# Encoder layer with two attention groups: the sample's queries rounded by GpSimd, its meta weights laid out by VectorE

## The chip, the cores and the metric

The kernel runs as one program on one core of a Trainium2 chip. The metric is the device time of one execution in microseconds (us), given as the median of several runs. The engines are TensorE (PE in the profile; PEld is its weight load), VectorE (DVE), ScalarE (ACT), GpSimd (POOL) and SyncE (SP), whose queue (SPq) issues the DMAs. Each engine works through its own list of instructions in order, and semaphores hold it where it needs another's result.

## The reference

One transformer layer is applied to a prompt of 1024 tokens and, on its own, to a sample of 512 tokens, both of width 1024 and with 16 learned meta tokens in front. Everything is float32.

```python
h = rmsnorm(x, norm1_g)
qa, ka, va, qb, kb, vb = split(h @ w_in)          # 8 heads of group A, 8 query heads of group B
qa, ka, qb, kb = (rmsnorm per head, with gains)
oa = neighbourhood_attn(qa, ka, va, rpb_a)        # 2-D window on the token grid, bias per offset
ob = windowed_gqa(qb, kb, vb, t5_table, sink_b)   # +-128 keys, 2 key heads, bias by distance, sink
x = x + concat(rmsnorm(oa), rmsnorm(ob)) @ w_out
x = x + (silu(h2 @ w_gate) * (h2 @ w_up)) @ w_down    # h2 = rmsnorm(x, norm2_g)
```

In both groups every query also attends to the 16 meta keys: a row of logits is the meta keys, the sink and up to 384 keys of the window. The softmax is taken over all of them together, and the output is the weighted sum of the values, those of the meta tokens included.

## The kernel before, in words

The program goes through stages: norm and projection of three segments of 512 tokens (two of the prompt, one of the sample), with the attention of the prompt behind the second segment and that of the sample behind the third; then the output projection and the feed-forward part for all twelve tiles of 128 tokens. The change lies in the attention of the sample, heads 16 to 31 in the kernel's count: 16 to 23 are group A, 24 to 31 group B. A head of the sample has four tiles of 128 queries, a head of the prompt eight. Tiles are numbered through: the sample's are 128 to 191. A group `g` is four tiles, so one head of the sample.

A float32 product is made exact enough by splitting each operand into a rounded high part (type fp32r) and a low part, the difference. A head's queries are therefore staged twice: the high part `qs[0]` by a copy (`stage_q` on ScalarE, L1251, or `raise_q` on GpSimd, L1001), and the low part by a subtraction (`lower_q` on GpSimd, L1008). The function `q_raised(h)` says which semaphore, and which value of it, tells that the high part of head `h` is there: `q_hi` for ScalarE's, `q_hi_pool` for GpSimd's. In the prompt GpSimd makes the high parts from the third head on. In the sample ScalarE makes all of them: three before the loop, and the other 13 in the loop, behind its work on the third tile of the head two before. When a high part is there, SP copies it by DMA to the other 64 partitions (`double_q`, L826).

For a tile, TensorE makes the scores (`scores`, L1988 to L1991), VectorE adds the bias and takes the maximum (`highest`, L1598), ScalarE the exponential (`exponent`, L1258), TensorE turns the weights (L1995), ScalarE rounds them (`raise_p`, L1267), VectorE makes their low parts (`lower_p`, L1605), and TensorE multiplies by the values (`values`, L2017). The weights of the 16 meta keys go another way, once per group: `keep_meta` (L1059) copies the first 16 columns of four tiles of `logit` into one tile `pmeta` of 64 columns; TensorE turns that (`turn_meta`, L2000), ScalarE and VectorE split it (L1275, L1612), and TensorE multiplies it by a block-diagonal matrix of the meta values (L2028), which GpSimd builds per head (`meta_values`, L1039).

The order on each engine is written out. In the sample GpSimd's turn for head `h` is: the meta weights of head `h - 1`; the masks of head `h + 2` (three additions of 128x256 or 128x384 in group A, L1030; single columns in group B, L1021 and L1022); the low part of the queries of head `h + 2`; the meta values of head `h + 1`; and on odd `h` the scaling of a finished pair of heads (`scale_pair`, L1047):

```python
if h > first:
    keep_meta(H.first // GROUP - 1)
...
if h + ahead < end:
    masks(h + ahead)
...
    lower_q(h + ahead)
if h + 1 < end:
    meta_values(h + 1)
```

SP's turn for head `h` is: the bias rows of head `h + 2` (L813 or L820), `double_q` of head `h + 2`, on even heads the store of a finished pair's sums (L831, behind ScalarE's copy at the head's fourth tile), on odd heads their load back in spread form (L839); four loads of the output weights stand between. TensorE's `turn_meta` for head `h` stands just in front of its scores for head `h + 2`. VectorE's `highest` at the first tile of a head's group waits for `meta_kept`, so that `logit` isn't overwritten early.

Of the kernel before, what the change touches and what calls it, by code (L numbers as in the profile page):

```python
# [19 lines left out]
META = 16  # L20
# [26 lines left out]
GROUP = 4  # L47
# [17 lines left out]
def hybrid_encoder_layer(nc, x_prompt, x_sample, meta_tokens, t5_table, norm1_g, w_in, qn_a_g, kn_a_g,  # L65
# [104 lines left out]
    logit = s("logit", [P, 2 * GROUP, KEYS])  # L170
# [8 lines left out]
    pmeta = s("pmeta", [P, 2, GROUP * META])  # L179
# [58 lines left out]
    with ExitStack() as ctx:  # L238
        bank = [ctx.enter_context(nc.psum_tensor(f"bank{i}", [P, 512], F32)) for i in range(8)]

        def sem(name):
            return ctx.enter_context(nc.semaphore(name))
# [45 lines left out]
        q_hi = sem("q_hi")  # L288
        q_hi_pool = sem("q_hi_pool")
# [5 lines left out]
        expd = sem("expd")  # L295
# [4 lines left out]
        meta_kept = sem("meta_kept")  # L300
        m_turned = sem("m_turned")
        m_hi = sem("m_hi")
        m_lo = sem("m_lo")
        vm_ready = sem("vm_ready")
# [8 lines left out]
        o_scaled = sem("o_scaled")  # L313
# [47 lines left out]
        def wait(eng, s, v):  # L361

            if not isinstance(v, int) or v > 0:
                eng.wait_ge(s, v)
# [19 lines left out]
        def f32(ap):  # L384
            return ap.bitcast(F32)
# [100 lines left out]
        def first_tile(h):  # L486
            return 8 * h if h < 16 else 128 + 4 * (h - 16)
# [122 lines left out]

        def q_raised(h):

            if 2 <= h < 16:
                return q_hi_pool, h - 1
            return q_hi, h + 1 if h < 2 else h - 13

        def double_count(h):

# [358 lines left out]
        def _(pool):  # L977
# [77 lines left out]
            def keep_meta(g):  # L1055
                pool.wait_ge(expd, GROUP * g + GROUP)
                wait(pool, m_turned, g - 1)
                first = GROUP * (g % 2)
                pool.tensor_copy(pmeta[:, g % 2, :].rearrange("p (t m) -> p t m", m=META),  # L1059
                                 logit[:, first:first + GROUP, 0:META]).then_inc(meta_kept, 1)  # L1060

            def attention(seq):
                first, end = HEADS_OF[seq]
                ahead = Head(first).ahead
                lower_q(first)
                pool.wait_ge(att_const, 16 * (first // 16 + 1))
                for h in range(first, first + ahead):
                    masks(h)
                    pool.wait_ge(bias_ready, h + 1)
                    lower_q(h + 1)  # L1070
                meta_values(first)
                for h in range(first, end):
                    H = Head(h)
                    if h > first:
                        keep_meta(H.first // GROUP - 1)
                    raised = first < h < end - ahead and q_raised(h + ahead)[0] is q_hi_pool
                    if raised:
                        pool.wait_ge(meta_kept, H.first // GROUP)
                        raise_q(h + ahead)
                        pool.wait_ge(*q_raised(h + ahead))  # L1080
                    if h + ahead < end:
                        masks(h + ahead)
                    if H.nt > GROUP:
                        keep_meta(H.first // GROUP)
                    if first < h < end - ahead:
                        pool.wait_ge(bias_ready, h + ahead + 1)
                        wait(pool, meta_kept, H.first // GROUP + 1 if H.nt > GROUP else 0)
# [3 lines that stand above are left out]
                    if seq == "prompt" and h % 2 == 0 and h >= 4:  # L1091
                        scale_pair(h // 2 - 2)
                    if h % 2 == 1 and h // 2 - ahead >= first // 2 and (seq == "sample" or h == end - 1):
                        scale_pair(h // 2 - ahead)
                keep_meta(first_tile(end) // GROUP - 1)
                for pair in range(end // 2 - ahead, end // 2):
                    if seq == "sample" and pair == end // 2 - 1:
                        for slot in range(2):
                            mix_lo(0, slot)
                    scale_pair(pair)  # L1100
# [395 lines left out]
        def _(dve):  # L1496
# [104 lines left out]
            def lower_p(n):  # L1601
# [3 lines left out]
                dve.tensor_tensor(turned_to(ptl, n), bank[2 + n % 2][:, 0:k * P].rearrange("p (k c) -> p k c", c=P),  # L1605
                                  f32(turned_to(pth, n)), ALU.subtract).then_inc(p_lo, 1)

            def lower_meta(g):
                pm = pmhl[:, g % 2, :]
                dve.wait_ge(m_hi, g + 1)  # L1610
                dve.wait_ge(p_hi, min(GROUP * g + 6, 128 if g < 32 else 192))
                dve.tensor_tensor(pm[64:P, :], bank[3][0:64, WIN:WIN + P], f32(pm[0:64, :]), ALU.subtract  # L1612
                                  ).then_inc(m_lo, 1)

            def attention(seq):
                n0, n1 = TILES[seq]
                first = HEADS_OF[seq][0]
                for i, q in enumerate(qs[seq]):
                    op = dve.memset(f32(q[1][64 - 64 * (i % 2):P - 64 * (i % 2), :]), 0.0)
                op.then_inc(q_zero, 1)  # L1620
                for h in (first, first + 1):
                    H = Head(h)
                    dve.wait_ge(*q_raised(h))
                    dve.tensor_copy(H.qs[0][H.other, :], H.qs[0][H.own, :]).then_inc(q_twin, 1)
                for h in range(first, first + Head(first).ahead + 1):
                    for k in range(3):
                        b_ = Head(h).bias_kind(k, MK)
                        dve.memset(b_[:, 0:META], 0.0)
                        op = dve.memset(b_[:, META:MK], MASKED)
                op.then_inc(b_zero, 1)  # L1630
                dve.wait_ge(b_zero, 1 if seq == "prompt" else 2)
                for n in range(n0, n1 + 9):
                    if n < n1:
                        highest(n)
                    if n % GROUP == 3 and n0 <= n - 7 < n1:
                        lower_meta((n - 7) // GROUP)
                    if n0 <= n - 2 < n1:
                        lower_p(n - 2)
                        h, t = where(n - 2)
                        if t == Head(h).nt - 1:  # L1640
                            dve.wait_ge(expd, n - 1)
                            wait(dve, rt_turned, h // 2)
                            c = h % 2 * (t + 1)
                            dve.reciprocal(rinv[:, c:c + t + 1], lsum[:, h % 2, 0:t + 1]).then_inc(inv_done, 1)
                    if n % GROUP == 0 and n0 <= n - 12 < n1:
                        h, t = where(n - 12)
                        dve.wait_ge(o_half, (n - 12) // GROUP + 1)
                        for src, dst in Head(h).o_parts(t // GROUP, 0):
                            op = dve.tensor_tensor(dst, src, dst, ALU.add)
                        op.then_inc(o_out, 1)  # L1650
# [604 lines left out]
```

## Time and profile before

| | us |
|---|---|
| median of 3 runs (2011.93 to 2013.73) | 2013.6 |
| the profiled execution | 2009.19 |
| its span, first to last instruction | 2007.4 |
| busy in the span: PE, DVE, ACT, POOL | 1865.8, 1291.5, 997.3, 953.8 |

The span is what the trace covers; the execution's own time has 1.8 us around it. All times in rows count from the span's start. The norm and projection of the prompt run to about 312 us, its attention to about 503, norm and projection of the sample to about 653, the sample's attention to about 768; output projection and feed-forward take the rest. A busy share over the whole span mixes these stages.

### The profile page before, as it was taken

What the parts mean: (1) busy time and instruction counts of PE and PEld (TensorE: products, weight loads), DVE (VectorE), ACT (ScalarE), POOL (GpSimd) and SP (SyncE); (2) the same over time, 40 slices, a digit from 0 to 9 for tenths busy, and PEclk for the clock granted to TensorE, in tenths of its full rate; (3) what the DMA queues carried; (4) which work ended last, traced back from release to release, by engine and by line L of the source; (5) the groups of instructions that cost most, each with busy time, mean ns of one, the idle gap of its engine ahead of it and who ended that gap; (6) DMA issues with size and microseconds to landing.
All of it is one profiled execution on the core that took longest, in us unless ns stands there. A gap on an engine that the chain in (4) does not pass through costs nothing.

```text
span 2007.4 us, 35821 instructions
## 1 busy us (share of the span) xinstructions
PE 1865.8 (93%) x12047; PEld 1678.2 (84%) x12047; DVE 1291.5 (64%) x2321; ACT 997.3 (50%) x2067; POOL 953.8 (48%) x823
## 2 busy tenths in 40 slices
PE   5995996999798788997899999999999999999998
PEld 3895776999576786886899999899999989999997
DVE  2665657888465666448666666776666676666664
ACT  3355346888444775335443544544444453544432
POOL 1331335765232753112654645555464564646543
PEclk9997998999799898999899999999999999999999
DMA  4442522444322445011323323252332325323221
GB/s 120 131 150 80 151 81 68 117 131 123 105 84 66 141 134 218 11 63 53 124 87 104 104 84 125 71 203 90 99 104 91 118 85 189 105 84 115 94 84 64
DMA packets 178796, 213.33 MB, mean 106 GB/s; under 512 B 12980, under 2 KB 157860, under 8 KB 178700
## 3 DMA queue, kind: packets, MB, share of 16 engines
q1 hardware_dynamic: 178700, 212.10, 33.3%
q8 instruction: 54, 0.88, 0.2%
q14 instruction: 42, 0.34, 0.1%
HBM read 195.76 MB, written 25.18 MB: 110 GB/s over the span
## 4 chain that ended last, share of the span: by engine, by line
PE 77%; issue 6%; DVE 5%; POOL 4%; ACT 3%; DMA 2%; SPq 1%; DVEq 0%; ACTq 0%; POOLq 0%
PE bank L380 22%; PE bank L382 21%; PE bank L381 21%; PE bank L2017 3%; PE bank L1995 2%; PE bank L1988 2%; PE bank L1941 1%; PE bank L1989 1%; POOL wl L984 1%; DVE mvl L1750 1%; PE bank L2028 1%; PE bank L1991 1%; POOL msl L1052 1%; DMA wraw<-in_w_in 1%; ACT msh L1327 0%
## 5 line engine op out<-in xcount | busy, mean ns | idle before, releaser
L380 PE MATMUL bank<-mvh,sth 128*128 128x256 f32 x1848 | 527.1, 285 | 16.6 <-DVE act_f L1766 5.6
L382 PE MATMUL bank<-mvh,stl 128*128 128x256 f32 x1848 | 526.0, 285 | 0.0
L381 PE MATMUL bank<-mvl,sth 128*128 128x256 f32 x1848 | 525.9, 285 | 0.0
L380 PEld LDWEIGHTS bank<-mvh,sth 128*128 128x128 f32 x1848 | 357.7, 194 | 19.6 <-issue 16.1
L381 PEld LDWEIGHTS bank<-mvl,sth 128*128 128x128 f32 x1848 | 357.8, 194 | 1.3
L382 PEld LDWEIGHTS bank<-mvh,stl 128*128 128x128 f32 x1848 | 357.6, 194 | 0.0
L1120 POOL TENSOR_TENSOR dl<-draw,dh 128x1024 fp32r<-128x1024 f32 x66 | 158.2, 2418 | 367.9 <-ACT dh L1420 367.9
L1788 DVE TENSOR_TENSOR y<-bank,y 128x512 f32<-128x512 f32 x264 | 182.4, 692 | 167.1 <-PE bank L382 166.2
L984 POOL TENSOR_TENSOR wl<-wraw,wh 128x1024 fp32r<-128x1024 f32 x54 | 132.4, 2454 | 275.9 <-ACT wh L1175 275.8
L1114 POOL TENSOR_TENSOR stl<-graw,sth 128x512 fp32r<-128x512 f32 x132 | 177.1, 1342 | 102.7 <-ACT sth L1402 99.4
L380 PE MATMUL bank<-dh,acth 128*128 128x512 f32 x528 | 211.0, 400 | 7.7 <-DVE y L1788 5.3
L381 PE MATMUL bank<-dl,acth 128*128 128x512 f32 x528 | 209.3, 396 | 0.0
L382 PE MATMUL bank<-dh,actl 128*128 128x512 f32 x528 | 209.2, 396 | 0.0
L380 PE MATMUL bank<-hth,wh 128*128 128x512 f32 (+2 forms) x512 | 199.6, 390 | 4.6 <-DVEq L375 3.8
L1436 ACT ACTIVATE acth<-act_f 128x512 fp32r<-128x512 f32 x66 | 38.2, 625 | 324.0 <-PE bank L382 315.9
L382 PE MATMUL bank<-hth,wl 128*128 128x512 f32 (+2 forms) x512 | 186.8, 365 | 0.0
L381 PE MATMUL bank<-htl,wh 128*128 128x512 f32 (+2 forms) x512 | 186.3, 364 | 0.0
L1114 POOL TENSOR_TENSOR stl<-uraw,sth 128x512 fp32r<-128x512 f32 x132 | 170.1, 1316 | 4.8 <-ACT sth L1402 4.8
L1556 DVE RECIPROCAL rt_p<-rt_p 128x512 f32<-128x512 f32 (+2 forms) x31 | 87.8, 2844 | 90.6 <-ACT rt_p L1228 90.6
L380 PEld LDWEIGHTS bank<-dh,acth 128*128 128x128 f32 x528 | 99.9, 189 | 31.3 <-DVE y L1788 6.3
L1258 ACT ACTIVATE logit<-logit,negm 128x274 f32<-128x274 f32 (+1 forms) x192 | 113.6, 592 | 20.9 <-DVE negm L1598 19.8
L380 PEld LDWEIGHTS bank<-hth,wh 128*128 128x128 f32 x512 | 98.2, 192 | 30.5 <-issue 6.3
(228 smaller groups left out, 4240.3 us busy)
## 6 DMA issues: line engine op xcount, KB each, us to landing
graw<-in_w_gate SPq DMA_DIRECT2D x33, 1024.0 KB, 5.2
uraw<-in_w_up SPq DMA_DIRECT2D x33, 1024.0 KB, 5.2
draw<-in_w_down SPq DMA_DIRECT2D x66, 512.0 KB, 4.1
wraw<-in_w_in SPq DMA_DIRECT2D x54, 512.0 KB, 3.8
bias_rows<-table_a SPq DMA_DIRECT2D x36, 192.0 KB, 3.1
out<-y SPq DMA_DIRECT2D x12, 512.0 KB, 3.1
bias<-table_b SPq DMA_DIRECT2D x28, 201.0 KB, 2.6
table_a<-line_a_dram SPq DMA_DIRECT2D x8, 576.0 KB
```

The source lines that it names most:

```text
L380: pe.matmul(out, lhs[0], rhs[0], start=start, stop=False, skip_group_check=True)
L381: pe.matmul(out, lhs[0], rhs[1], start=False, stop=False, skip_group_check=True)
L382: return pe.matmul(out, lhs[1], rhs[0], start=False, stop=stop, skip_group_check=True)
L984: pool.tensor_tensor(wl[slot][:, :, :], wraw[slot][:, :, :], f32(wh[slot][:, :, :]), ALU.subtract).then_inc(w_lo, 1)
L1114: pool.tensor_tensor(stl[:, i, :, :], standing(raw, i), f32(sth[:, i, :, :]), ALU.subtract).then_inc(st_lo_pool, 1)
L1120: pool.tensor_tensor(dl[j][:, :], draw[j][:, :], f32(dh[j][:, :]), ALU.subtract).then_inc(down_lo, 1)
L1258: act.activation(x, x, ACT.Exp, bias=negm[:, h % 2, t:t + 1], scale=-1.0, accum_out=lsum[:, h % 2, t:t + 1]).then_inc(expd, 1)
L1556: op = dve.reciprocal(rt[slot][:, u0:u0 + w], rt[slot][:, u0:u0 + w])
L1788: dve.tensor_tensor(yt, DOWN_BANK[half][:, :], yt, ALU.add).then_inc(y_add, 1)
L1988: pe.matmul(S[:, MK:H.width(t)], q[0], win, start=True, stop=False, skip_group_check=True)
L1995: return pe.transpose(bank[2 + n % 2][:, c * P:(c + 1) * P], logit[:, n % (2 * GROUP), MK + c * P:MK + (c + 1) * P], ident[:, :])
L2017: return pe.matmul(H.o_bank(t // GROUP)[0:cols, c:c + len(ts) * P], H.v_block(b)[:, 0:cols], w, start=fresh, stop=False, skip_group_check= ...
```

## The change

Two edits, both for the sample alone. First, `q_raised` sends heads 19 to 31 to GpSimd: heads 16 to 18 stay with ScalarE (they are staged before the loop), and in GpSimd's turn for head `h` a `raise_q(h + 2)` now stands in front of the masks, with two waits of its own (`vm_ready`, `o_scaled`). ScalarE's `stage_q` in the loop falls away, since it asks `q_raised`. Second, GpSimd's `keep_meta` is made for the prompt alone, and VectorE gets a `keep_meta` of its own, one `tensor_copy` per head of the sample, behind the low part (`lower_p`) of the head's last tile and the reciprocal of its sums, and in front of `highest` of the next tile. TensorE's `turn_meta` waits for the same semaphore as before.

```diff
         def q_raised(h):
-            if 2 <= h < 16:
+            if h < 2:
+                return q_hi, h + 1
+            if h < 16:
                 return q_hi_pool, h - 1
-            return q_hi, h + 1 if h < 2 else h - 13
+            return (q_hi, h - 13) if h < 19 else (q_hi_pool, h - 4)
...
-                    if h > first:
+                    if h > first and seq == "prompt":
                         keep_meta(H.first // GROUP - 1)
                     raised = first < h < end - ahead and q_raised(h + ahead)[0] is q_hi_pool
                     if raised:
-                        pool.wait_ge(meta_kept, H.first // GROUP)
+                        if seq == "prompt":
+                            pool.wait_ge(meta_kept, H.first // GROUP)
+                        else:
+                            pool.wait_ge(vm_ready, h + 1)
+                            pool.wait_ge(o_scaled, max(8, h // 2 - 2))
                         raise_q(h + ahead)
                         pool.wait_ge(*q_raised(h + ahead))
...
-                keep_meta(first_tile(end) // GROUP - 1)
+                if seq == "prompt":
+                    keep_meta(first_tile(end) // GROUP - 1)
...
+            def keep_meta(g):
+
+                dve.wait_ge(expd, GROUP * g + GROUP)
+                wait(dve, m_turned, g - 1)
+                first = GROUP * (g % 2)
+                dve.tensor_copy(pmeta[:, g % 2, :].rearrange("p (t m) -> p t m", m=META),
+                                logit[:, first:first + GROUP, 0:META]).then_inc(meta_kept, 1)
...
+                    if seq == "sample" and n % GROUP == 1 and n0 <= n - 5 < n1:
+                        keep_meta((n - 5) // GROUP)
                     if n % GROUP == 0 and n0 <= n - 12 < n1:
```

## Rows read from the trace of the kernel before

**Rows 1.** The chain that ended last, 658 to 768 us: shares by line.
```profile
by line: issue 20.7%; PE bank L2017 7.8%; PE bank L1995 6.0%; POOL kall L1008 5.8%; POOL spare L1030 5.7%; DMA spare<-table_a 3.8%; POOL bd L1039 3.6%; POOL qm L1047 3.4%; ACT logit L1258 3.0%; PE bank L1988 3.0%; DMA spare<-table_b 2.7%; P
```

**Rows 2.** Waits, 655 to 790 us: total us, times, longest us.
```profile
ACT pmhl L1275 <- PE bank L2000: 13.4, 8, 2.3
...
PE bank L2000 <- POOL pmeta L1059: 10.6, 8, 2.0
```

**Rows 3.** Timeline of PE: start us, us, instruction, idle before it and releaser.
```profile
668.18 0.27 PE L2000 MATMUL bank<-ident,pmeta 128*64 128x128 f32 x1 [1.77 <-POOL pmeta L1059]
...
703.29 0.27 PE L2000 MATMUL bank<-ident,pmeta 128*64 128x128 f32 x1 [2.00 <-POOL pmeta L1059]
...
716.44 0.27 PE L2000 MATMUL bank<-ident,pmeta 128*64 128x128 f32 x1 [0.39 <-POOL pmeta L1059]
...
722.01 0.27 PE L2000 MATMUL bank<-ident,pmeta 128*64 128x128 f32 x1
729.14 0.27 PE L2000 MATMUL bank<-ident,pmeta 128*64 128x128 f32 x1 [1.15 <-POOL pmeta L1059]
...
756.19 0.27 PE L2000 MATMUL bank<-ident,pmeta 128*64 128x128 f32 x1
...
756.86 0.33 PE L1988 MATMUL bank<-kall 128*128 128x256 f32 x1
...
761.55 0.27 PE L2000 MATMUL bank<-ident,pmeta 128*64 128x128 f32 x1
```

**Rows 4.** Stretches: length, busy us of PE, PEld, DVE, ACT, POOL; clock, DMA share, GB/s.
```profile
706.00:708.00 2.00, 2.00 (x14) 2.00 (x14) 1.68 (x5) 1.79 (x5) 1.92 (x4) 0.50 0.60 130
...
730.00:732.00 2.00, 2.00 (x17) 1.92 (x17) 1.20 (x4) 2.00 (x7) 0.00 (x0) 1.00 0.58 211
```

**Rows 5.** Timeline of POOL, columns as in rows 3.
```profile
667.23 0.62 POOL L1039 TENSOR_TENSOR bd<-vml,block 128x256 fp32r<-128x256 f32 x1
...
667.98 2.39 POOL L1030 TENSOR_TENSOR bias<-spare,mask_a 128x256 f32<-128x256 f32 x3
670.45 1.27 POOL L1008 TENSOR_TENSOR kall<-qm,kall 64x512 fp32r<-64x512 f32 x1
671.81 0.61 POOL L1039 TENSOR_TENSOR kall<-vmh,block 128x256 fp32r<-128x256 f32 x1
...
696.75 2.39 POOL L1030 TENSOR_TENSOR spare<-spare,mask_a 128x256 f32<-128x256 f32 x3 [1.56 <-DMA spare<-table_a]
699.21 1.28 POOL L1008 TENSOR_TENSOR kall<-qm,kall 64x512 fp32r<-64x512 f32 x1
```

**Rows 6.** Instructions of L1001 (the prompt's heads): ns min/median/max, first and last start.
```profile
L1001 POOL CAST qs_p0h<-qm x14: 609/610/613, 331.9 to 469.4; 64x512 fp32r<-64x512 f32 x14
```

**Rows 7.** L1251, columns as in rows 6; and L1059's group, 658 to 768 us.
```profile
L1251 ACT ACTIVATE kall<-qm x8: 617/627/631, 654.4 to 751.3; 64x512 fp32r<-64x512 f32 x8
...
L1059 POOL COPY pmeta<-logit 128x64 f32<-128x64 f32 x16 | 3.9, 242 | 4.9 <-ACT logit L1258 4.9
```

**Rows 8.** SP's own waits, 655 to 770 us; and one of its issues.
```profile
SPq L826 <- ACT kall L1251: 28.3, 8, 7.2
SPq L826 <- ACT qs_s1h L1251: 14.0, 3, 5.3
...
SPq L826 <- ACT qs_s0h L1251: 11.0, 3, 4.5
...
691.51 1.40 SPq L813 DMA_DIRECT2D spare<-table_a  x3
```

**Rows 9.** Timelines of POOL and DVE before the first tile of the sample.
```profile
655.22 2.74 POOL L1030 TENSOR_TENSOR bias<-bias_rows,mask_a 128x256 f32<-128x256 f32 x3
...
655.71 0.52 DVE L1624 CAST qs_s0h<-qs_s0h 64x512 fp32r<-64x512 f32 x1
656.26 1.11 DVE L1624 CAST qs_s1h<-qs_s1h 64x512 fp32r<-64x512 f32 x1
657.32 0.07 DVE L1628 MEMSET bias<- 128x16 f32 x1
```

## Prediction

> **What bounds the kernel now.** I read the page first: its chain of waits is TensorE matmul nearly everywhere, and the change touches none of that. So I went to the one stage that it does touch, the sample's attention (about 658 to 768 us), and took its chain alone. There the reader is to see that TensorE no longer leads: GpSimd lines (L1008, L1030, L1039, L1047) and the DMAs of the bias rows stand in it beside the matmuls [rows 1]. The view of waits says where the two meet: TensorE waited eight times, 10.6 us in all, at `turn_meta` (L2000) for GpSimd's copy of the meta weights (L1059), and ScalarE behind it 13.4 us [rows 2]. The copy itself is short; it is late because it stands in GpSimd's queue behind the masks, the low parts and the scaling of other heads.
>
> Next the pace. L2000 runs once per head. From the first (668.18) to the fifteenth (761.55) [rows 3] are 14 heads in 93.4 us, 6.67 each. Where nothing held TensorE a head took 5.57 us (716.44 to 722.01), and 5.36 (756.19 to 761.55) in the last heads, where ScalarE has no queries left to round [rows 3]. So over 1.1 us per head is waiting or what follows it. What follows is the clock: after the 2.00 us wait before 703.29 [rows 3] the granted clock stands at 0.50 (1.2 GHz) from 706 to 708 us, while after the 1.15 us wait before 729.14 it stays at 1.00 (2.4 GHz) [rows 4]. A wait near 2 us costs more than itself; one near 1 us does not.
>
> **The change part by part.**
>
> *Meta weights to VectorE.* GpSimd loses 16 copies, 3.9 us in all [rows 7], and with them the wait for the exponentials at the start of each turn. TensorE's wait at L2000 for GpSimd goes. What is late next there: VectorE makes the copy right behind `lower_p` of the head's last tile, for which TensorE waits at L2000 anyway, so the copy is TensorE's only if it takes longer than the matmuls in front of L2000. The two waits that VectorE gets are met on arrival: the exponential precedes the rounding that `lower_p` just waited for, and `m_turned` is a head old. Queued behind the copy on VectorE is `highest` of the tile after next, and ScalarE's exponential behind that. The trace has no such copy on VectorE. From below: a 128x16 memset took 0.07 us [rows 9]; a gain below that is excluded, since VectorE shows no wait for GpSimd's copies. From above: a 64x512 copy between SBUF buffers took 0.52 us once and 1.11 us the next time, both beside GpSimd's masks [rows 9]. I take 0.2 us, nearer to the lower end because the copy has 64 elements per partition, and keep 1.11 for the range.
>
> The same pair of rows shows that a VectorE copy beside GpSimd can take over twice its time. The Trainium skill ("SBUF — State Buffer", section "Who interferes with whom") says why: the two engines share one pair of SBUF ports as an exclusive lock, a VectorE copy in a two-port mode takes it, and whoever comes second blocks until the other's instruction ends. No other VectorE operation of this loop reads SBUF alone, so the copy would be the first to meet this lock; by that rule each of the 16 would be held as in the second rival below, and the time would be that rival's.
>
> *Queries to GpSimd.* ScalarE loses 13 roundings of 0.627 us [rows 7], 8.2 us in all. The rows of the pace show what that is worth where ScalarE is in the ring: 5.57 against 5.36, 0.2 us per head, and I let the 0.2 of the copy eat it. GpSimd gains 13 of 0.61 us (the prompt's form has two such instructions per head, the sample's one) [rows 6] and the gap of 0.08 that its instructions show between a result and its use (670.37 to 670.45, [rows 5]). The two added waits, `vm_ready` and `o_scaled`, are on semaphores that GpSimd raised itself earlier; they cost that gap and no more. Queued behind them are the masks and low parts of the head two ahead.
>
> *SP's queue.* The load of the other half of the queries stands in SP's queue in front of the next head's bias load, and SP stood there 53.3 us in 14 waits (28.3, 14.0, 11.0) for ScalarE's rounding [rows 8]. Now GpSimd rounds first in its turn, before the masks, so the transfer starts earlier, and on odd heads the bias load behind it too. On even heads SP still waits next for the sums that ScalarE copies out at the head's fourth tile.
>
> *The sum.* In the first half (2-D attention) GpSimd sets the pace; its masks take 2.39 us there. It ends `meta_values` of head 17 at 667.85 [rows 5]. From there to the low part of head 23 come five roundings (0.69 with the gap), five masks (2.47), five low parts (1.36) and four `meta_values` (1.17 each, two instructions): 3.5 + 12.3 + 6.8 + 4.7 = 27.3 us. To that come waits for bias rows. Before, the load for head 23 was issued at 691.51 and its masks began at 696.75 [rows 5, 8]; ScalarE will be some 4 us earlier at the point that released it, so the rows land about 692.8, 0.8 us after GpSimd is done rounding. The same reckoning gives 0.7 for the other four together. Bounds: nothing, and five times the 1.56 us that this mask waited before [rows 5], 7.8. With 1.5 the low part of head 23 is ready at 696.65 instead of 700.49. TensorE would be there at 666.41 + 0.67 + 5 x 5.57 = 694.9 (its first L2000 without the 1.77 us wait, and 0.67 from an L2000 to the next scores, 756.19 to 756.86 [rows 3]), so GpSimd decides, by waits that are under 1 us per head and leave the clock alone. Before, head 23's scores began at 703.29 + 0.67 = 703.96. Gained by here: 7.3 us.
>
> From head 23 to head 31 masks are single columns, and GpSimd has room. Before: 756.86 - 703.96 = 52.9 us. After: 8 x 5.57 = 44.6, which gains 8.3; I take back 0.8 for one late bias load behind an output weight load on SP (bounds nothing and the same 1.56). Nothing after head 31's first score changes: the tail, output projection and FFN shift as they are. Sum: 7.3 + 8.3 - 0.8 = 14.8 us. The profiled execution, 2009.2 us (span 2007.4 and 1.8 around it), would take 1994.4. The median of the runs is 4.4 above that execution; the same difference on the median, 2013.6, gives **1998.8 us**.
>
> **The rivals.**
>
> *The engines' own pace.* GpSimd is never late, and a head takes 5.36. Head 23 at 695.2, then 8 x 5.36 = 42.9: 8.8 + 10.0 = 18.8 us, 1994.8. For it: the last heads ran so. Against: 27.3 us of GpSimd work without any wait.
>
> *The copy on VectorE is held by GpSimd.* The price of a hold is 1.11 - 0.52 = 0.59 us. GpSimd is busy through most of a turn, so each head pays it: 6.16 instead of 5.57, and the eight late heads gain 3.6 instead of 8.3. With 7.3 from the first half and 0.8 back, about 10 us: 2003.5. For it: the two casts. Against: VectorE idles around that place, and ScalarE has lost 0.63 us just behind it.
>
> *Bias rows bound GpSimd.* SP's order keeps their loads late, the masks wait 7.8 us instead of 1.5, and the first half gains 1.0: 8.5 us in all, 2005.1.
>
> *GpSimd's longer turn sets every head (slower).* Its chain from one head to the next already filled 6.67 us, waits included. If the rounding does not fill those waits, because bias load and double now both hang on it through SP, the turn grows by 0.69 - 0.24 = 0.45 us in 13 heads: TensorE waits for the low queries instead of the meta weights, 5.9 us slower, 2019.5. It decides if a turn stays over 6.67. For it: GpSimd in the stage's chain. Against: the masks wait for DMA exactly where the rounding now stands, and the work alone is 5.7 us per turn.
>
> *The wait only changes its name.* L2000 also waits for `lower_p`; if that was as late as the copy, TensorE stands there as long and the time stays at 2013.6. Against: in the free heads L2000 came with no wait at all.
>
> **How the numbers follow.** Forecast 0.50, own pace 0.08, held copy 0.20, bias rows 0.10, longer turn 0.07, renamed wait 0.05. The range reaches from 1994 (own pace, a little over) to 2007 (past the held copy and the bias rows) and leaves the last two out. Two runs of this kernel tell a difference of about 0.2%, 4 us: faster 0.88, the same 0.05, slower 0.07.
>
> **What would show it.** The L2000 rows have no GpSimd in front of them, and their spacing is 5.4 to 6.0 us in the first half and 5.4 to 5.7 in the second. The granted clock is 1.00 throughout from 670 us. What waits for GpSimd, if anything, are scores (L1988) of heads 20 to 23, by about a microsecond. SP's waits for ScalarE's rounding are gone. The stage ends some 15 us earlier and the stages behind it keep their lengths. I am wrong if the new VectorE copy takes over 0.5 us in most heads, if L2000 rows stay above 6.3 us apart, or if low queries or bias rows hold TensorE or VectorE in most heads.

## The result, and the profile after

The changed kernel takes 1998.89 us (median of 11 runs, 1992.96 to 2004.77); the kernel before, on the same chips, takes 2011.93 us (11 runs, 2005.43 to 2014.61). The ratio is 0.994, with a 95% interval of 0.9926 to 0.9954, so the change is faster by 13.0 us. The forecast was 1998.8 us. The total hides an error: VectorE's copy took nearly three times what was assumed for it. A difference of 1.4 us outside the stage and the scatter of the medians covered that.

In the profiled executions the span fell from 2007.4 to 1994.7 us. To keep the stage apart from the rest of the program, the text below measures it from GpSimd's first low part of the sample (`lower_q`, 653.89 us before, 654.93 after) to ScalarE's first copy for the output projection (`msh`, 768.30 and 758.03). So measured the stage fell from 114.41 to 103.10 us, 11.3 less. The other 1.4 us of the span lie outside: the stage began 1.0 later and what follows it was 2.4 shorter, in code that the change doesn't touch. Over the executions shown here the stage's start lies anywhere from 653.4 to 656.3 us, so a difference of this size outside the stage can't be put down to the change.

The lines of the changed kernel are 2 to 17 higher: `turn_meta` is L2017 now, `scores` L2005, `highest` L1605, GpSimd's rounding L1003, its low part L1010, its masks L1032 (group A) and L1023 and L1024 (group B), and VectorE's new copy L1620. First the waits of the changed kernel, 655 to 775 us (total us, times, longest us):

```profile
ACT logit L1265 <- DVE negm L1605: 13.5, 23, 2.2
...
POOL bias L1023 <- DMA bias<-table_b: 5.6, 2, 3.6
...
PE bank L2017 <- DVE pmeta L1620: 3.5, 7, 0.7
...
PE bank L2005 <- POOL kall L1010: 1.3, 2, 1.0
...
PE bank L2005 <- POOL qs_s1l L1010: 0.9, 1, 0.9
```

TensorE's 10.6 us at `turn_meta` for GpSimd [rows 2] are gone, and 3.5 us for VectorE's copy stand in their place, none over 0.71. The timeline of PE (start, us, instruction, idle before it) shows where:

```profile
679.21 0.39 PE L2005 MATMUL bank<-kall,qs_s0h 128*128 128x256 f32 x1 [0.19 <-POOL qs_s0l L1010]
...
685.51 0.39 PE L2005 MATMUL bank<-kall,qs_s1h 128*128 128x256 f32 x1 [0.93 <-POOL qs_s1l L1010]
...
692.04 0.39 PE L2005 MATMUL bank<-kall 128*128 128x256 f32 x1 [0.98 <-POOL kall L1010]
...
697.01 0.27 PE L2017 MATMUL bank<-ident,pmeta 128*64 128x128 f32 x1 [0.28 <-DVE pmeta L1620]
...
698.21 0.39 PE L2005 MATMUL bank<-kall 128*128 128x256 f32 x1 [0.36 <-POOL kall L1010]
...
732.30 0.27 PE L2017 MATMUL bank<-ident,pmeta 128*64 128x128 f32 x1 [0.68 <-DVE pmeta L1620]
...
738.47 0.27 PE L2017 MATMUL bank<-ident,pmeta 128*64 128x128 f32 x1 [0.46 <-DVE pmeta L1620]
...
744.85 0.27 PE L2017 MATMUL bank<-ident,pmeta 128*64 128x128 f32 x1 [0.68 <-DVE pmeta L1620]
...
755.67 0.27 PE L2017 MATMUL bank<-ident,pmeta 128*64 128x128 f32 x1 [0.71 <-DVE pmeta L1620]
```

In the first half the scores of heads 20 to 23 wait for GpSimd's low parts, 0.19, 0.93, 0.98 and 0.36 us, as forecast. In the second half `turn_meta` waits for the new copy. From the first `turn_meta` (667.26) to the fifteenth (750.40) a head takes 5.94 us, against 6.67 before [rows 3]. The granted clock, which had been 0.50 from 706 to 708 us [rows 4], is 1.00 there and in every other stretch of 2 us from 666 to 760. The columns of the stretches (length, busy us of PE, PEld, DVE, ACT, POOL, clock, DMA share, GB/s) are those of before:

```profile
706.00:708.00 2.00, 1.78 (x17) 1.78 (x18) 1.94 (x6) 1.66 (x5) 1.50 (x7) 1.00 0.52 134
730.00:732.00 2.00, 1.62 (x15) 1.42 (x13) 1.97 (x6) 1.09 (x4) 2.00 (x3) 1.00 0.87 205
```

VectorE is now busy in 1.94 and 1.97 of 2.00 us there, against 1.68 and 1.20 [rows 4]. The same times hold other work in the two kernels, so this is no measure by itself, and about half of the 1.97 is one long copy. The new copy in the view of groups by shape (count, busy us, mean ns):

```profile
L1620 DVE COPY pmeta<-logit 128x64 f32<-128x64 f32 x16 | 9.2, 574 | 0.0
```

The mean of 574 ns is of unlike instructions: four of the sixteen took 0.16 us, eight over 0.5, the longest 1.13. The timelines of DVE and of POOL around two long ones and two short ones say what makes the difference:

```profile
677.76 0.16 DVE L1620 COPY pmeta<-logit 128x64 f32<-128x64 f32 x1
...
731.02 1.13 DVE L1620 COPY pmeta<-logit 128x64 f32<-128x64 f32 x1
732.07 0.56 DVE L1605 CUSTOM_DVE_ANT_0 logit<-bank,bias 128x402 f32<-128x402 f32 x1
...
749.77 0.16 DVE L1620 COPY pmeta<-logit 128x64 f32<-128x64 f32 x1
...
754.51 1.00 DVE L1620 COPY pmeta<-logit 128x64 f32<-128x64 f32 x1
```
```profile
675.42 2.39 POOL L1032 TENSOR_TENSOR spare<-bias_rows,mask_a 128x256 f32<-128x256 f32 x3
...
730.83 1.27 POOL L1049 TENSOR_TENSOR qm<-qm,rinv_q 128x512 f32<-128x512 f32 x1
...
754.20 1.27 POOL L1049 TENSOR_TENSOR qm<-qm,rinv_q 128x512 f32<-128x512 f32 x1 [7.17 <-DVE qm L1666]
```

The copy at 749.77 had no GpSimd instruction beside it and took 0.16 us. So did the one at 677.76, which came just before GpSimd's masks ended (677.81). The one at 731.02 came 0.19 us into GpSimd's scaling (730.83 to 732.10) and ended at 732.15; the one at 754.51 came into the scaling that ended at 755.47 and ended at 755.51. So a copy that comes while GpSimd's instruction runs ends with it. The traces bear this out copy by copy: in the change and in e1, e8 and e9 below, which have the same copy, every copy that took 0.19 us or more ended 0.04 to 0.06 us after the single GpSimd instruction in which it had begun. The others took 0.15 to 0.17 us: they had no GpSimd instruction beside them, or one with little of its time left. The text calls such a copy held. `highest` then starts late, and ScalarE's exponential behind it:

```profile
732.68 0.63 ACT L1265 ACTIVATE logit<-logit,negm 128x402 f32<-128x402 f32 x1 [0.97 <-DVE negm L1605]
```

ScalarE's waits for `highest`, 23 and 13.5 us in the first fence, were these in the same stretch of the kernel before:

```profile
ACT logit L1258 <- DVE negm L1598: 6.7, 15, 2.2
```

In e4 to e7 below, where the copy is not held, they are 6.7 to 7.7 us in 15 waits again, as in e6:

```profile
ACT logit L1265 <- DVE negm L1605: 7.7, 15, 2.2
```

### The profile page after: what moved, and what is told of

Its sections match the earlier page's. It is cut to its first block, busy times and chain, and to the rows that moved or that the text cites. A ratio compares the mean times of both kernels' runs of the same rounds, so it can differ in the third digit from the quotient of the medians.

```text
span 1994.7 us, 35834 instructions
## 1 busy us (share of the span) xinstructions
PE 1857.7 (93%) x12047; PEld 1671.4 (84%) x12047; DVE 1298.8 (65%) x2337; ACT 989.4 (50%) x2054; POOL 957.3 (48%) x820
## 4 chain that ended last, share of the span: by engine, by line
PE 77%; DVE 6%; issue 6%; POOL 3%; ACT 3%; DMA 2%; SPq 2%; DVEq 0%; ACTq 0%; POOLq 0%
PE bank L380 22%; PE bank L381 21%; PE bank L382 21%; PE bank L2034 3%; PE bank L2012 2%; PE bank L2005 2%; PE bank L1958 1%; PE bank L2006 1%; POOL wl L986 1%; DVE mvl L1767 1%; PE bank L2045 1%; PE bank L2008 1%; POOL msl L1054 1%; ACT msh L1334 0%; DVE tsum L1763 0%
```

## The experiments

Ten kernels ran on three chips: four beside a kernel before of 2009.74 us, four beside 2010.01 us, two beside 2011.16 us. The stage's length is that of the one profiled execution, whose time stands beside it, since it can lie some microseconds from the median (4.2 above for e1, 4.4 below for e9).

| kernel | median us | ratio to before (95%) | profiled execution us | its stage us | VectorE copy, mean ns |
|---|---|---|---|---|---|
| before | 2011.93 | 1 | 2009.19 | 114.41 | none |
| the change | 1998.89 | 0.9940 (0.9926 to 0.9954) | 1996.55 | 103.10 | 574 |
| e1_copy_alone | 2000.89 | 0.9956 (0.9939 to 0.9973) | 2005.07 | 107.28 | 553 |
| e2_queries_alone | 2005.35 | 0.9975 (0.9961 to 0.9989) | 2005.47 | 112.90 | none |
| e3_copy_on_scalar | 1995.39 | 0.9918 (0.9895 to 0.9941) | 1998.25 | 102.87 | none (ScalarE: 248) |
| e4_copy_unheld | 1995.01 | 0.9923 (0.9901 to 0.9944) | 1994.85 | 102.68 | 184 |
| e5_unheld_scalar_q | 1996.82 | 0.9937 (0.9920 to 0.9953) | 1995.32 | 99.88 | 186 |
| e6_unheld_wo_later | 1995.26 | 0.9924 (0.9906 to 0.9941) | 1994.37 | 100.11 | 185 |
| e7_mixed_queries | 1992.45 | 0.9913 (0.9895 to 0.9930) | 1994.33 | 97.09 | 185 |
| e8_held_wo_later | 1997.26 | 0.9939 (0.9922 to 0.9955) | 1995.39 | 101.21 | 414 |
| e9_change_beside_mixed | 2000.06 | 0.9943 (0.9929 to 0.9958) | 1995.71 | 102.75 | 542 |
| e10_mixed_beside_change | 1994.69 | 0.9910 (0.9895 to 0.9924) | 1995.56 | 97.98 | 185 |

### Each edit alone

**The copy alone.** From the changed kernel, the queries go back to ScalarE:

```diff
-            if h < 2:
-                return q_hi, h + 1
-            if h < 16:
+            if 2 <= h < 16:
                 return q_hi_pool, h - 1
-            return (q_hi, h - 13) if h < 19 else (q_hi_pool, h - 4)
+            return q_hi, h + 1 if h < 2 else h - 13
```

> VectorE copies the meta weights as in the changed kernel, but ScalarE rounds the sample's queries as before. The stage is measured from GpSimd's first low part of the sample to ScalarE's first high part of the output projection: 114.4 us before, 103.1 with the whole change. Theory 'the copy's place is the gain': TensorE no longer waits for GpSimd at the turn of the meta weights, the stage takes 103 to 106 us and the execution is 8 to 12 us faster than before; since GpSimd has 0.69 us less to do per head, scores don't wait for its low parts in heads 20 to 23. Rival 'the queries are the gain' (ScalarE relieved, SP's queue freed): the stage stays above 109 us and the time within 5 us of before.

It is 8.9 us faster than before, as forecast, but the stage, 107.28 us, is longer than the 103 to 106 forecast; its profiled execution lies 4.2 us above the median. No score waits for GpSimd's low parts; `turn_meta` waits for the copy instead, as the group by shape and the waits (total us, times, longest us) show:

```profile
L1618 DVE COPY pmeta<-logit 128x64 f32<-128x64 f32 x16 | 8.9, 553 | 0.0
```
```profile
PE bank L2015 <- DVE pmeta L1618: 3.4, 10, 0.8
```

So the copy's move is the larger part of the change, two thirds of the 13.0 us, and VectorE's copy is held with ScalarE's rounding as well as with GpSimd's.

**The queries alone.** The kernel before, with the new `q_raised` alone. GpSimd's turn asks it, so `raise_q(h + 2)` now stands in front of the masks, behind the copy that is still GpSimd's:

```diff
-            if 2 <= h < 16:
+            if h < 2:
+                return q_hi, h + 1
+            if h < 16:
                 return q_hi_pool, h - 1
-            return q_hi, h + 1 if h < 2 else h - 13
+            return (q_hi, h - 13) if h < 19 else (q_hi_pool, h - 4)
```

> GpSimd rounds the sample's queries as in the changed kernel, but also still copies the meta weights at the start of its turn. Theory 'the copy's place is the gain': nothing is gained; GpSimd's turn grows by about 0.7 us in 13 heads, part of it filled by waits for bias rows, so TensorE waits longer at the turn of the meta weights than the 10.6 us of before, the stage takes 114 to 121 us and the time lies 0 to 7 us above before. Rival 'the queries are the gain': ScalarE's 8 us and the earlier bias loads shorten the stage to 104 to 109 us, 5 to 10 us faster.

That forecast fell: it is not slower, but 4.4 us faster by the medians (0.25%, interval 0.11% to 0.39%). The rival's stage of 104 to 109 us did not come either: in the profile the stage is only 1.5 us shorter, a head takes 6.56 us, and TensorE still stands at `turn_meta` (L2002 here) for GpSimd. The waits, the timeline of PE and the stretches behind its longest wait:

```profile
PE bank L2002 <- POOL pmeta L1061: 10.1, 8, 3.0
...
POOL pmeta L1061 <- ACT logit L1260: 4.9, 2, 3.9
```
```profile
703.67 0.39 PE L2002 MATMUL bank<-ident,pmeta 128*64 128x128 f32 x1 [3.00 <-POOL pmeta L1061]
```
```profile
704.00:706.00 2.00, 2.00 (x12) 2.00 (x11) 0.25 (x1) 1.00 (x4) 1.86 (x8) 0.50 0.28 63
706.00:708.00 2.00, 2.00 (x10) 1.93 (x10) 0.95 (x4) 0.70 (x4) 1.86 (x5) 0.50 0.05 10
```

Ten microseconds of waiting and the low clock (1.2 GHz) behind it are those of the kernel before. What moved the median by the other 3 us isn't in the stage of this one execution, and stays open. What falls is the rival of the longer turn: GpSimd's added rounding did not make the turn longer, 6.56 us against 6.67.

### The hold, taken away in two ways

**The copy on ScalarE** (248 ns each, behind its rounding of the head's last weights), GpSimd rounding the queries as in the change:

```diff
+                act.activation(pmeta[:, g % 2, :].rearrange("p (t m) -> p t m", m=META),
+                               logit[:, first:first + GROUP, 0:META], ACT.Copy).then_inc(meta_kept, 1)
...
                         raise_p(n - 1)
+                    if seq == "sample" and n % GROUP == 0 and n0 <= n - 4 < n1:
+                        keep_meta((n - 4) // GROUP)
...
-                dve.tensor_copy(pmeta[:, g % 2, :].rearrange("p (t m) -> p t m", m=META),
-                                logit[:, first:first + GROUP, 0:META]).then_inc(meta_kept, 1)
```

> The whole change, but ScalarE makes the copy of the meta weights (behind its rounding of the head's last tile), not VectorE. Theory 'held copy' (VectorE's copy took 0.16 us where GpSimd was idle and up to 1.13 where it was busy, and the hold delays the loop): a ScalarE copy takes about 0.25 us always, TensorE's 3.5 us of waits for the copy go, and the stage falls from 103.1 to 99 to 102 us. Rival 'the hold is hidden in VectorE's idle time': ScalarE pays 0.25 us per head that it had not, and the stage takes 103 to 106 us.

No wait for the copy is left at `turn_meta`. In exchange the scores wait for GpSimd's low parts up to 1.83 us in the first half and 2.02 us at head 30, where one turn takes 8.92 us. The stage, 102.87 us, lies between the two forecasts and is hardly shorter than the change's in this execution, yet the median is 14.4 us below before.

**The copy in another form on VectorE**: the sum over an axis of length one, which gives the same values:

```diff
-                dve.tensor_copy(pmeta[:, g % 2, :].rearrange("p (t m) -> p t m", m=META),
-                                logit[:, first:first + GROUP, 0:META]).then_inc(meta_kept, 1)
+                dve.tensor_reduce(pmeta[:, g % 2, :].rearrange("p (t m) -> p t m", m=META),
+                                  logit[:, first:first + GROUP, 0:META].rearrange("p t (m o) -> p t m o", o=1),
+                                  mybir.AxisListType.X, ALU.add).then_inc(meta_kept, 1)
```

> The whole change, with VectorE's copy written as a reduction over an axis of length one: the same 64 elements on the same engine at the same place, but a different instruction. Theory 'held copy', by the lock that only two-port copies take: each takes about 0.2 us whatever GpSimd does, TensorE's waits for it go, and the stage falls by 1 to 3 us to 100 to 102 us. Rival 'VectorE is held by something else (its own order, or any read beside GpSimd)': the instruction keeps taking 0.2 to 1.1 us and the stage stays at 103 us. Rival 'the hold is hidden': the instruction takes 0.2 us, and the stage stays at 103 us all the same.

This form is not held, in none of its 16 instructions:

```profile
L1620 DVE TENSOR_REDUCE pmeta<-logit 128x64 f32<-128x64 f32 x16 | 2.9, 184 | 0.0
```

The Trainium skill ("SBUF — State Buffer", section "Who interferes with whom") has copies among the VectorE operations that can take the ports shared with GpSimd, and says that a `tensor_reduce` on this chip never contends for them. The rows agree with both: 0.16 to 1.13 us for the one, 0.18 to 0.19 us throughout for the other, on the same 64 elements at the same place.

The heads then run 5.35 to 5.65 us apart, except where the scores of heads 22 and 23 wait 0.66 and 0.96 us for low parts, and at head 30, where a new wait appears. The timelines of PE, of POOL and of SP's queue lead from the wait to its cause:

```profile
739.80 0.39 PE L2006 MATMUL bank<-kall 128*128 128x256 f32 x1 [2.52 <-POOL kall L1010]
```
```profile
737.88 0.18 POOL L1023 COPY bias<-sink 128x1 f32<-128x1 f32 x1 [4.33 <-DMA bias<-table_b]
```
```profile
731.19 0.58 SPq L804 DMA_DIRECT2D wo_early<-in_w_out  x1
731.82 1.38 SPq L822 DMA_DIRECT2D bias<-table_b  x3
```

The bias rows of head 30 were issued right behind an output-weight load, and landed 4.33 us after GpSimd wanted them; that turn takes 9.39 us, with the clock at 0.50 from 742 to 744 us. By its own stage, 102.68 us against 103.10, e4 would leave the rival of the hidden hold standing; this one turn is some 4 us longer than its neighbours and covers the gain. This is the late bias load to which the prediction gave 0.8 us. The change has the same wait on GpSimd (3.56 of the 5.6 us in the first fence), but TensorE, slowed by held copies, comes later there and shows no wait for the low part.

### Unheld, with the queries rounded by either engine

**e4's copy, with ScalarE's rounding as in e1:**

> VectorE lays out the meta weights with the reduction of length one, which took 0.18 us beside GpSimd, and ScalarE rounds the queries as before. With the plain copy and ScalarE's queries the stage took 107.3 us (107.3 against 103.1 with GpSimd's queries). Theory 'the queries matter for ScalarE': without any hold the ring of ScalarE and VectorE still has 0.5 us more per head in 13 heads where ScalarE rounds, and the stage takes 103 to 106 us. Rival 'they only mattered because the held copy and ScalarE's rounding fall into the same place': the stage takes 101 to 103 us, as with GpSimd's queries. Rival 'SP': bias rows come later behind ScalarE's rounding, and scores or maxima of heads 20 to 23 wait for masks; the stage takes over 106 us.

The stage is 99.88 us, below what any of the three gave. Turns run from 5.49 to 5.94 us, no score waits for a low part, and the clock is 1.00. Against e1, where only the form of the copy differs, the stage is 7.4 us shorter, but those two profiled executions lie on either side of their medians. By the medians' distance from before (8.9 us for e1, 13.2 for this) the hold is worth 4.3 us there.

**e4 with two output-weight loads moved behind the late bias loads:**

```diff
-                    if h in (25, 27):
+                    if h in (29, 30):
                         sp.wait_ge(bias_ready, 24)
-                        wo_load(0 if h == 25 else 1)
+                        wo_load(0 if h == 29 else 1)
```

> The change with the unheld copy, and the two output-weight loads that stand in SP's queue in its turns for heads 25 and 27 moved to those for heads 29 and 30. With the loads in their old place TensorE waited 2.5 us for the low part of head 30 and ran at the low clock after it; that turn took 9.4 us instead of 5.5. Theory 'the output-weight load makes head 30's bias late': the wait goes, no turn of the second half is over 5.8 us, the clock stays at 1.00, and the stage falls from 102.7 to 98.5 to 99.5 us. Rival 'GpSimd or SP's order is late there anyway': a wait of over 1.5 us for a low part stays in heads 28 to 31 and the stage stays above 101 us.

The wait at head 30 is gone and every turn of the second half takes 5.35 to 5.46 us. That settles its cause. But in the first half one wait of 1.51 us at head 23 is followed by the low clock, and that turn takes 8.56 us, so the stage, 100.11 us, misses the forecast. The timeline of PE and the stretches show it (the medians, 0.9923 and 0.9924 of before, don't tell e4 from e6):

```profile
700.02 0.39 PE L2006 MATMUL bank<-kall 128*128 128x256 f32 x1 [1.51 <-POOL kall L1010]
```
```profile
700.00:702.00 2.00, 1.98 (x11) 1.92 (x12) 0.65 (x3) 0.00 (x0) 1.96 (x3) 0.65 0.21 63
702.00:704.00 2.00, 2.00 (x12) 2.00 (x11) 1.16 (x2) 1.75 (x6) 1.74 (x9) 0.50 0.00 0
```

**The change itself with that move of the loads, its copy held:**

> The whole change as it is, with VectorE's plain copy, and only the output-weight loads moved to the turns for heads 29 and 30. Beside the run with the unheld copy and the same loads it gives the price of the hold without the late head 30. Theory 'held copy': no low part was late with the held copy, so the move alone gives nothing (102 to 103.5 us for the stage), and the unheld copy is worth 3 to 4.5 us. Rival 'the hold is mostly hidden': the two runs' stages are within 1 us of each other.

The stage is 101.21 us, below the 102 to 103.5 forecast: its sixteen copies were shorter than the change's, 414 ns on average against 574, and whether the move of the loads did that is not shown. It is 1.1 us longer than e6's, near what the rival gave, but e6 has its one slow turn, worth 3.2 us (8.56 against 5.4). In the seven turns from head 22 to head 29 no score waits for a low part in e6, e8 or the change. They take 5.39 us in e6, 5.61 in e8 and 5.90 in the change (from `turn_meta` to `turn_meta`, 706.21 to 743.97, 702.40 to 741.66, 703.55 to 744.85), with copies of 0.19, 0.39 and 0.69 us on average. There a turn grows by as much as its copy does.

Three pairs of kernels now differ by the hold alone, and three by the engine that rounds the queries. The ratios to before give each pair's difference (x 2010 us); beside it stands what the medians' distances to before give:

| pair | ratios | difference us | by medians us |
|---|---|---|---|
| hold: e1, e5 (ScalarE rounds) | 0.9956, 0.9937 | 3.8 | 4.3 |
| hold: the change, e4 (GpSimd rounds) | 0.9940, 0.9923 | 3.4 | 1.7 |
| hold: e8, e6 (GpSimd rounds, loads moved) | 0.9939, 0.9924 | 3.0 | 2.0 |
| queries: before, e2 (GpSimd copies) | 1, 0.9975 | 5.0 | 4.4 |
| queries: e1, the change (copy held) | 0.9956, 0.9940 | 3.2 | 4.2 |
| queries: e5, e4 (copy unheld) | 0.9937, 0.9923 | 2.8 | 1.5 |

No difference but that of e2 is clear of its own interval (each ratio has about 0.0016 to either side), but all six point the same way. The hold costs some 2 to 4 us whichever engine rounds, and the move of the queries gains some 2 to 5 us beside it; no closer figure is shown. By the medians the two edits add up, 4.4 + 8.9 = 13.3 us against 13.0.

### The better version

**e6, with ScalarE rounding the queries of heads 19 to 23, and GpSimd those of heads 24 to 31**, where its masks are single columns and it has time:

```diff
-            return (q_hi, h - 13) if h < 19 else (q_hi_pool, h - 4)
+            return (q_hi, h - 13) if h < 24 else (q_hi_pool, h - 9)
```

> As the run with the output-weight loads later and the unheld copy, but ScalarE rounds the queries of heads 19 to 23 and GpSimd those of 24 to 31. Theory 'GpSimd's work sets the pace in the first half': its turn is 0.69 us shorter there, scores of heads 20 to 23 don't wait for it (they waited 1.6 us), and the stage falls by 1 to 2 us below the other run's. Rival 'SP's order': bias rows stand behind ScalarE's rounding again, masks come later by more than the 0.69 us, and the stage is 0 to 3 us longer.

The stage is 97.09 us, 3.0 less than e6's, with turns of 5.36 to 5.95 us, no wait for a low part and a clock of 1.00. That is more than the theory gave, since e6's slow turn is gone too. The medians don't tell it from e6: the intervals of the two ratios overlap. It was then run again beside the change:

> The changed kernel itself, on one chip with the mixed version. Both theories of the copy expect what its own runs showed: 0.993 to 0.995 of before, a stage of 102 to 104 us, copies between 0.16 and 1.1 us.

> The mixed version (unheld copy, output-weight loads later, ScalarE rounding heads 19 to 23 and GpSimd 24 to 31) beside the change on one chip. If its 97.1 us stage is its own and not one execution's luck, the stage takes 96.5 to 98 us again, no turn over 6 us and the clock at 1.00, and the execution is 4 to 7 us faster than the change's. Rival 'it was the execution': a wait of over 1.3 us for a low part and a stretch at the lower clock come back, and the two are within 3 us.

On this chip the change takes 2000.06 us and this version 1994.69, 5.4 us less, with intervals of the ratio that don't meet (0.9929 to 0.9958 and 0.9895 to 0.9924). Its stage was 97.98 us this time. The forecast that no turn takes over 6 us fell: bias rows came late for head 22, TensorE waited 1.62 us for its low part, and that turn took 7.00 us. The clock stayed at 1.00, as the timelines of POOL and PE and the stretch behind the wait show:

```profile
687.86 2.39 POOL L1032 TENSOR_TENSOR bias<-bias_rows,mask_a 128x256 f32<-128x256 f32 x3 [2.82 <-DMA bias_rows<-table_a]
```
```profile
691.63 0.39 PE L2006 MATMUL bank<-kall 128*128 128x256 f32 x1 [1.62 <-POOL kall L1010]
```
```profile
692.00:694.00 2.00, 2.00 (x21) 2.00 (x20) 0.96 (x3) 1.02 (x3) 2.00 (x4) 1.00 0.51 120
```

## Why the prediction was right, and where it was not

**The mechanism was the one named.** The wait at `turn_meta` for GpSimd went, the low clock behind it went, and the pace fell under 6 us. Of the medians' 13.0 us, the copy alone brings 8.9 (e1) and the queries alone 4.4 (e2); the prediction had not divided its sum so. It put the queries at 0.2 us a head and set the copy against that.

**The sum had 14.8 us, the stage gave 11.3.** The missing 3.5 us can be placed by three marks of the same two timelines, taking the stage's later start of 1.04 us off:

| stretch | before | after | forecast gain | gain |
|---|---|---|---|---|
| stage's start to head 23's scores | 50.07 | 43.28 | 7.3 | 6.8 |
| head 23's scores to head 31's | 52.90 | 47.31 | 8.3 - 0.8 | 5.6 |
| head 31's scores to the stage's end | 11.44 | 12.51 | 0 | -1.1 |

**First half, 0.5 us short.** The low part of head 23 was forecast at 696.65, which is 697.69 with the later start; it ended at 698.16. The rows of POOL that answer to [rows 5]:

```profile
693.32 0.61 POOL L1003 CAST kall<-qm 64x512 fp32r<-64x512 f32 x1
694.43 2.39 POOL L1032 TENSOR_TENSOR spare<-spare,mask_a 128x256 f32<-128x256 f32 x3 [0.50 <-POOL kall L1003]
696.89 1.27 POOL L1010 TENSOR_TENSOR kall<-qm,kall 64x512 fp32r<-64x512 f32 x1
```

Rounding, masks and low part took what the sum gave them. The waits in front of the masks made 2.0 us (0.62, 0.89, 0.50) where 1.5 were allowed, and that is the 0.5. The releaser named for the last of them is GpSimd's own rounding, which ended at 693.93. By the chain of waits the head's bias rows, whose last part was issued at 689.83 and took 4.10 us, landed at the same moment. The forecast had 692.8, which is 693.84 with the later start, so these rows came when it said. GpSimd was late by the two waits before, which made 1.51 us where 0.7 were allowed for four.

**The copy, the term that was mis-sized.** It was taken as 0.2 us, from the lower end of a range whose upper end was 1.11 [rows 9], with the reason that it has only 64 elements. Its length has little to do with its elements: 0.16 us alone, up to 1.13 us beside GpSimd (1.25 in e1). The two casts of [rows 9] had shown it. Taken one by one, the masks beside them end at 655.95 and 657.08, and the casts end 0.28 and 0.29 us after those, at 656.23 and 657.37. So both were held, and 1.11 - 0.52 is not the price of a hold. Nor was it only the copy that "reads SBUF alone": the reciprocal of the sums does too, but took 0.16 to 0.17 us each time.

The argument against a hold, that VectorE idles around that place, was wrong by the trace of before. There `highest` starts right behind the reciprocal, with no gap in 14 of 15 heads, here in the timeline of DVE before the change:

```profile
721.53 0.16 DVE L1644 RECIPROCAL rinv<-lsum 128x4 f32<-128x4 f32 x1
721.61 0.54 DVE L1598 CUSTOM_DVE_ANT_0 logit<-bank,bias 128x402 f32<-128x402 f32 x1
```

A copy put between the two pushes `highest` back by its whole length, and in the changed kernel `highest` follows the copy with no gap in all 15. In the second half the turns that end with a copy of over 1 us take 6.17 to 6.39 us, those with one of 0.16 to 0.20 us 5.36 to 5.55. Of the 1.1 us of the tail 0.9 is the same thing. Nothing was forecast behind head 31's first score, but the last head's copy (754.51, 1.00 us) is held too, by a scaling for which VectorE itself gave the signal 0.4 us earlier (it ended L1666 at 754.06), and the last turn takes 5.27 us instead of 4.39. Second half and tail together lost 3.0 of the 3.5 us, and the pairs above, which take the hold away, give 1.7 to 4.3 back.

**The held-copy rival was the true mechanism, on top of a pace that was taken too slow.** It put the hold at 0.59 us in each of the eight late heads and the whole at 10 us gained; 11.3 us were gained in the stage. The copies of the eight turns between head 23's scores and head 31's took 0.72 us on average, 0.56 above the 0.16 of a copy alone, so the size of the hold was right. What the rival, and the forecast with it, had wrong is the pace without a hold: 5.57 us a head, where unheld heads take 5.39 (e6). The change's 5.91 is that pace and a hold of about 0.5. So the hold costs some 4 us in these eight heads and 0.9 in the tail, and the shortfall looks smaller than that because the pace under it was better than forecast and the late bias load cost nothing.

**The late bias load** (0.8 us) was there on GpSimd's side, 3.56 us long, and cost TensorE nothing in this execution, which came there late by its held copies; when the change ran again (e9), TensorE waited 0.63 us for the low part of head 30. Once they are unheld it costs a turn of 9.39 us (e4), and goes with the loads' place in SP's queue (e6).

**SP's waits for the rounding are not gone, only shorter.** The prediction had them gone. The queue's own view answers to [rows 8]:

```profile
SPq L828 <- POOL kall L1003: 20.8, 7, 5.5
...
SPq L828 <- POOL qs_s0h L1003: 9.3, 3, 4.1
SPq L828 <- POOL qs_s1h L1003: 7.9, 3, 3.5
```

38.0 us for GpSimd's rounding, against 53.3 for ScalarE's: SP still arrives first and stands, but it is let go earlier: the bias rows of head 23 are issued from 688.86 on instead of 691.51, 3.7 us earlier in the stage, about the 4 us that the sum had used.

**Longer turn, renamed wait, bias rows.** The first fell with e2. The second came true in part, for another reason than its own: TensorE waits 3.5 us, where it had waited 10.6, at the same line for VectorE. But the releaser is the held copy and not a late `lower_p`, since with the unheld copy (e4 to e7) nothing waits there at all. The third did not decide: the masks of the first half waited 2.0 us, not 7.8.

**Why the median came out so near.** The profiled execution was forecast at 1994.4 us and took 1996.55. The stage's shortfall of 3.5 us was covered in part by the 1.4 us outside it. The forecast for the median then put 4.4 us on top, from three runs of before that lay high; the median lies 2.3 us above the profiled execution, and that made up the other 2.1. That the forecast was met to 0.1 us is luck; the mechanism and the first half of the sum are not.

## What to carry to other kernels

A copy between SBUF buffers that moves from GpSimd to VectorE must be priced beside what GpSimd does at that moment, not by its size: here 0.16 us alone and up to 1.13 us beside a 1.27 us instruction. A form that isn't held (a sum over an axis of length one, 184 ns) won back some 2 to 4 us. When an engine is made faster, look again at the loads behind it in the queue: a bias load behind a weight load cost TensorE at most 0.6 us until the heads ran at 5.4 us, and then 4 us in one turn. And where two engines can do a piece of work, a split by stretch of the loop is worth a try: ScalarE's rounding in the first half and GpSimd's in the second, with the unheld copy and the moved loads, took 5.4 us off the change. What the split alone gives is not shown.

## What the runs showed of the hardware

A strided copy on VectorE of only 64 elements per partition (four pieces of 16) is held until the GpSimd instruction in which it began has ended, and no longer: where the next GpSimd instruction followed without a gap, the copy still ended 0.05 us after the first (e.g. the copy at 743.58 of the change, which ended at 744.71, with GpSimd's scaling ending at 744.65). The Trainium skill ("Perfetto Trace Analysis", section "Optimizing Scalar/DVE Operations") warns that moving work between GpSimd and VectorE might not help for this reason. Here the move was worth 8.9 us in spite of it (e1): in GpSimd's queue the copy stood behind other heads' work, and TensorE waited 10.6 us for it, against 3.4 in e1.

The length of a wait alone did not settle whether the clock fell behind it. It went to 0.50 (1.2 GHz) behind a wait of 1.51 us (e6) and of 3.00 us (e2), and stayed at 1.00 (2.4 GHz) behind one of 1.62 us (e10) and one of 1.83 us (e3). So the prediction's "a wait near 2 us costs more than itself; one near 1 us does not" holds for its own two rows, but between them the runs show both.
